# Three products of constants ahead of each wait for normalised attention weights

## The reference

```python
def block(inp):
    ql, qr, qp = inp
    s = jnp.einsum("bqhr,bkr->bhqk", ql, kv) + jnp.einsum("bqhd,bkd->bhqk", qr, kr)
    s = s.astype(jnp.float32) * MLA_SCALE
    s = jnp.where(k_pos[None, None, None, :] <= qp[None, None, :, None], s, -jnp.inf)
    p = jax.nn.softmax(s, axis=-1).astype(kv.dtype)
    return jnp.einsum("bhqk,bkr->bqhr", p, kv)
```

## Time and profile before

| What | Value |
|---|---|
| median of 3 executions | 2383.07 us |
| the profiled execution, its span | 2382.49 us, 2380.7 us |
| TensorE busy (matmul) | 2054.9 us, 86% of the span |
| VectorE, ScalarE, GpSimd busy | 946.1, 773.8, 654.3 us |
| mean granted clock of TensorE | 0.875 |

### The profile page before, as it was taken

How to read it: one execution, slowest core, us unless ns; L and a number is a source line. 1 busy time by engine, 2 the same in 40 slices (tenths; PEclk the granted TensorE clock), 3 DMA queues, 4 the chain that set the end, 5 groups by cost and what they waited for, 6 DMA issues and landing times. The chain is left out here.

```text
span 2380.7 us, 39144 instructions
## 1 busy us (share of the span) xinstructions
PE 2054.9 (86%) x16191; PEld 1864.0 (78%) x16191; DVE 946.1 (40%) x1477; ACT 773.8 (33%) x1395; POOL 654.3 (27%) x332
## 2 busy tenths in 40 slices
PE   4998887589779999989959987847979899999996
PEld 3997654468778999989859965536868799999995
DVE  2332433744332333345426044365433133333553
ACT  4333223243242322233344241323332422222433
POOL 0341100511222344434214310023103223443440
PEclk8998756589789999999979976656989999999998
DMA  2431001145012223222032210030722032322210
GB/s 88 136 63 38 7 5 59 44 175 195 29 56 75 86 71 106 70 92 98 10 104 89 28 44 0 6 102 6 281 87 71 28 106 72 101 75 97 76 63 38
DMA packets 168754, 177.23 MB, mean 74 GB/s; under 512 B 47198, under 2 KB 151302, under 8 KB 166340
## 3 DMA queue, kind: packets, MB, share of 16 engines
q1 hardware_dynamic: 163884, 132.58, 18.2%
q0 software_dynamic: 4608, 41.95, 4.8%
q10 hardware_dynamic: 100, 0.46, 0.1%
HBM read 166.11 MB, written 8.86 MB: 73 GB/s over the span
## 5 line engine op out<-in xcount | busy, mean ns | idle before, releaser
L337 POOL TENSOR_TENSOR w_low<-ring,w_high 128x1024 fp32r<-128x1024 f32 x120 | 290.7, 2424 | 613.8 <-ACT w_high L333 613.8
L356 PE MATMUL ps<-x_high,w_high 128*128 128x272 f32 x1664 | 346.7, 290 | 28.3 <-DVE x_low L347 22.3
L333 ACT ACTIVATE w_high<-ring 128x1024 fp32r<-128x1024 f32 x166 | 174.8, 1055 | 537.3 <-PE ps L356 483.1
L356 PE MATMUL ps<-x_low,w_high 128*128 128x272 f32 x1664 | 343.3, 287 | 0.0
L356 PE MATMUL ps<-x_high,w_low 128*128 128x272 f32 x1664 | 342.1, 287 | 0.0
L356 PEld LDWEIGHTS ps<-x_high,w_high 128*128 128x128 f32 x1664 | 260.8, 189 | 30.0 <-DVE x_low L347 23.2
L356 PEld LDWEIGHTS ps<-x_low,w_high 128*128 128x128 f32 x1664 | 262.6, 189 | 0.0
L356 PEld LDWEIGHTS ps<-x_high,w_low 128*128 128x128 f32 x1664 | 261.6, 188 | 0.0
L356 PE MATMUL ps<-x_high_in,w_high 128*128 128x272 f32 x736 | 154.1, 291 | 45.3 <-POOL w_low_in L337 45.3
L2532 DVE TENSOR_SCALAR arena<-arena,parb 128x560 f32<-128x560 f32 x44 | 84.4, 1919 | 271.4 <-ACT arena L2480 271.4
L337 POOL TENSOR_TENSOR w_low_in<-ring,w_high 128x1024 fp32r<-128x1024 f32 x46 | 109.8, 2389 | 271.5 <-ACT w_high L333 271.5
(11 more groups left out here) (398 smaller groups left out, 3517.4 us busy)
## 6 DMA issues: line engine op xcount, KB each, us to landing
ring<-in_ffn_w_up SPq DMA_DIRECT2D x44, 1024.0 KB, 5.5
ring<-in_ffn_w_down SPq DMA_DIRECT2D x20, 1024.0 KB, 5.1
ring<-in_w_in SPq DMA_DIRECT2D x18, 1024.0 KB, 5.3
ring<-in_w_out SPq DMA_DIRECT2D x8, 1024.0 KB, 8.1
ring<-in_ple_w_gate SPq DMA_DIRECT2D x8, 1024.0 KB, 5.2
big<-in_state_ssm SPq DMA_DIRECT2D x16, 256.0 KB, 4.2
out_ssm_sample<-big SPq DMA_DIRECT2D x4, 1024.0 KB
arena<-in_x_prompt SPq DMA_DIRECT2D x1, 2048.0 KB
```

What stands on the lines that cost most here:

```text
L333: act.activation(wh[:, i % 2], ring[:, n % RING, :, c0:c0 + P], ACT.Copy).then_inc(s_high, 1)
L337: pool.tensor_tensor(low[:, i % 2], ring[:, n % RING, :, c0:c0 + P], wh[:, i % 2].bitcast(F32), ALU.subtract).then_inc(s_low, 1)
L356: last = pe.matmul(ps[:, b + h, 0:HALF], w[:, i % 2, k, :], x[:, k, h * HALF:(h + 1) * HALF], start=(k == 0 and x is x_high and w is wh), ...
```

## The change

Ahead of each of the 11 waits for normalised weights TensorE gets three float32 products: the 128 x 128 identity is held, the first 256 columns of the constant `sel` (zeros, with a one here and there) pass through, and the result goes to bank 6, which the transposes behind the wait overwrite. Nothing reads it. The wait for `s_ptk`, which protects bank 6, now stands ahead of the products; the wait for `s_pn` stands behind them.

```diff
+                    def keep_running(bank, n):
+
+                        for _ in range(n):
+                            pe.matmul(ps[:, bank, 0:256], ident, C("sel")[:, 0:256], start=True, stop=True)
+
                     def probs_across(i):
-                        e.wait_ge(s_pn, i + 1)
                         if i:
                             e.wait_ge(s_ptk, i)
+                        keep_running(B_M + 1, 3)
+                        e.wait_ge(s_pn, i + 1)
                         for k in range(step_cols(i) // P):
                             last = pe.transpose(ps[:, B_M + 1, k * P:(k + 1) * P], Pp[:, i % 2, k * P:(k + 1) * P], ident)
                         last.then_inc(s_pt, 1)
```

## The result

The changed kernel takes 2366.68 us (median of seven, 2358.34 to 2372.38) against 2384.95 for the kernel before in the same runs (2381.78 to 2389.39): a ratio of 0.9921, 95% interval 0.9902 to 0.9939. The forecast was 2366. The profiled execution took 2367.72 us.

What follows compares the result with a forecast made beforehand. TensorE at mean clock 0.67 was taken to bound the two layers' stages. 9.2 us saved less 0.85 lost gave 8.35 a layer, 16.7 in two, from 2382.49 to 2365.8, or 2366 on the runs' scale; range 2335 to 2390.

Steps and rivals of the forecast that it cites:

- The rival in which the products only cost: All eleven places: sparse products leave the clock as it is and cost 13.1 us a layer, 2409 us; chance 0.13.
- idle time alone loses the clock: Skill's rule for TensorE: only the waits of steps 0 to 4 lose the clock, giving the outcome of the first rival.
- The first rival: Both halves of the stage: clock held nearly everywhere, up to 32 us a layer saved, 2342 to 2319 us; chance 0.17.
- The price: Each of the eleven places: three products take 1.4 us at full clock, 2.5 at half.
- Steps 0 to 4: First half: products run inside VectorE's waits and keep the clock behind them, 9.2 us a layer saved.
- the idle time left over: Waits of steps 0 to 4: 1.5 to 3.0 us remain at steps 0, 1, 2, 4; short ones keep the clock.
- the small L859: Behind step 2: narrow work of 32 columns, 3.62 us, in which the clock was expected to fall.
- The bound: First half: largest possible saving, 17.7 us a layer, with the small L859 included.
- The reading of narrow work: Before the change, at 353.3: clock fell after 3.30 of 3.30 busy us, mostly 32-row scores, so narrow work loses it.
- Steps 5 to 10: Second half: products cost 8.45 us, a higher clock returns 7.6, so 0.85 us a layer lost.
- step 10: Second half: products pay nothing, since L1036 waits 1.70 us behind them for ScalarE's copy.
- The give-back: Second half: wide products raise the clock for 17.2 us of work at half clock, 7.6 us a layer returned.

Runs made afterwards that it cites:

- e3: Changed kernel with the three products at all eleven places cut to 32 of 128 rows, same length in time: 2421.99 us, ratio 1.0146 to the kernel before.
- e7: Changed kernel with full operands (triangular constant held, cosines passed through) in all eleven places: 2366.01 us, ratio 0.991 to the kernel before.
- e8: Changed kernel with twelve 128 x 128 transposes instead of three products, only ahead of steps 0 to 4: 2349.06 us, ratio 0.9856 to the kernel before.
- e6: Changed kernel with one product instead of three, only ahead of steps 0 to 4: 2364.25 us, ratio 0.9915 to the kernel before.
- e5: Changed kernel with 6, 8, 6, 3 and 9 products ahead of steps 0 to 4, none later: 2344.97 us, ratio 0.9831 to the kernel before.
- e1: Changed kernel with its three products only ahead of steps 0 to 4, none later: 2347.29 us against 2384.72 for the kernel before, ratio 0.9853.

## Why the prediction was right, and where it was not

The mechanism is shown: the gain is the clock, kept by wide work in the waits. Filling the same waits with narrow work of the same length gave nothing there (e3), and dense operands (e7) and transposes (e8) did as well as the change's products. The rival in which the products only cost (2409) did not come, and what it describes is what e3 did. That idle time alone loses the clock is refuted by e3 too. The first rival, the clock held nearly everywhere (2342 to 2319), did not come either: in layer 0 the mean clock is 0.81 in the first half and 0.71 in the second.

That the time came out within 1 us of the forecast is partly luck. The two stages gained 10.8 and 7.8 us where 8.35 each was forecast, with parts that err both ways, and about 4 us were lost outside them.

**The price.** 1.4 us for three at full clock was 1.30 to 1.48, 2.5 at half was 2.56 to 2.72. For steps 5 to 9 the sum was 8.45, less the 0.18 of waiting at step 6; the trace has 8.47, or 8.29 with that taken off.

**Steps 0 to 4.** 9.2 us were taken; 12.9 and 10.2 came. The total is near, its parts are not. From one step's transposes to the next, before and after: step 0 to 1 took 15.39, now 10.79 (gained 4.6; predicted 4.3); 1 to 2 took 15.78, now 11.32 (4.5) in layer 0, and in layer 1 15.67 and 14.20 (1.5); 2 to 3 took 13.17, now 12.58 (0.6; predicted 3.3 less 0.5); 3 to 4, measured to 331.88, took 15.81, now 12.60 (3.2; for this one and 1 to 2 together 2.1 was predicted). The failed step is that the idle time left over decides whether the clock is kept. Step 1, which the forecast counted for a quarter only, kept it with 2.55 us left in layer 0, and lost it with the same 2.55 in layer 1:

```profile
1435.74 0.66 PE L1030 MATMUL ps<-cst,ring 128*128 128x128 f32 x4 [2.55 <-DVE ring L1305]
...
1437.39 1.05 PE L1012 MATMUL ps<-big,ring 128*128 128x256 f32 x2
```

Behind step 2, with 1.82 left, it fell at 294.1, 5 us ahead of the small L859 where the prediction expected it, and so took most of the 3.3 us with it. The 32-row scores had begun only 0.1 us earlier, and in e7's layer 1 the clock outlasted them and L859, so their being narrow is not what decided. e6 shows places that differ in the same way. From step 3 to 4 the gain is that the clock was up from 307.9, behind step 3's products; the prediction had these down as a cost of 0.5, and a quarter of the stretch behind them as gained. The bound was about right: 17.7 us for the whole half, and e5, which leaves next to nothing idle, gained 18.7 (73.9 to 55.2).

**The reading of narrow work.** The prediction laid the fall at 353.3 to narrow work, and counted five long stretches at half the clock where the earlier trace rows has six of 10 us or more. In the changed kernel the same instructions (L1015, L920, L911, L920) run from 336.98 to 339.75 inside the window 331.80:358.90, and the clock stays at 1.00. So one such stretch does not show that narrow work loses the clock; e3 does, where narrow products stand in place of wide ones in every wait.

**Steps 5 to 10.** 0.85 us lost was predicted, 2.1 and 2.0 came, since step 10 paid 1.7 where nothing was taken: at half the clock three products outlast ScalarE's 1.70. The prediction had a price for it (1.4), but only in a rival. The give-back then is 8.3 + 1.7 - 2.1 = 7.9, and 7.6 was taken. What the prediction did not see is that this is no fair account: with the first half held, the second half without products is 1.5 to 4.3 us shorter than before the change (e1), so in these traces the products there lose 6.4 us in layer 0 and 3.5 in layer 1 against the kernel that leaves them out.

**The rest.** The two stages together gave about 19 us in the profiled executions, whose whole times differ by 14.8. The remaining 4 us went between the stages: from the start of the GLA stage in layer 0 (L1637) to the first score of the next layer it took 1008.7 us before and 1013.6 after, with the same instructions. The runs of one kernel spread over 5 to 17 us here, so no cause is put to it; why the same code finds the clock at one level in one layer or run and at the other in the next is open, and was not tried.

## What to carry over

Where a trace shows TensorE at half its clock behind a wait that another engine ends, try wide throw-away products in that wait, short enough not to outlast it: here they bought back 37 us. Ahead of every such product ask what TensorE would have done in its place, since where it did not wait they cost more than they returned (4 to 19 us). The busy share is not enough to judge by: fillers of 32 rows kept TensorE as busy in the waits as those of 128 rows, and the clock fell (e3). And cut the stage where the waits stop before summing up: with the products of both halves 18 of the 37 us were left.

## What had not been expected of the hardware

- Idle time of 2.51 us lost the clock and 2.69 kept it, at two places of one kernel and in both layers (e6); and at one place of one kernel 1.82 us lost it in layer 0 and 1.83 kept it in layer 1 (e7).
- Twelve 128 x 128 transposes of a constant keep the clock as well as three products of 256 columns (2349 and 2347 us).
- Operands of zeros and of cosines are the same to it (2367 and 2366 us).
- With narrow fillers the clock fell below what it had been without any (0.57 against 0.63 in the second half), so busy narrow time is not neutral. That it takes the place of wider work is one reading, which no run tests.
